# A second load of the keys in groups of 512 columns, and two steps of ScalarE in another order

## What is computed

```python
mix = concat([o_att, o_conv], -1) @ w_out
x1  = layer_norm(ALPHA * x + gate1 * mix)
h2  = x1 * (1 + scale2) + shift2
q   = (h2 @ w_pq).reshape(T, 8, 2, 128)
s   = einsum('thpd,hpnd->thpn', q, sub_keys)      # merged: h2 @ m, m is 1024 x 2048
sv, si = top_k(s, 16)                             # per head and half
cv, ci = top_k(all 256 sums of the two halves, 16)
e   = expert numbers from si and ci               # 8 heads x 16 = 128 per token
a   = gelu(einsum('thkd,td->thk', peer_u[e], h2))
f   = einsum('thk,thkd->td', softmax(cv) * a, peer_v[e])
y   = layer_norm(ALPHA * x1 + gate2 * f)
```

## Time and profile before

| | |
|---|---|
| median of 3 runs | 3889.26 us (3885.03 to 3895.07) |
| profiled execution, own time | 3891.0 us |
| its span, first to last instruction | 3889.2 us |
| busy: PE, DVE, POOL, ACT | 3238.2, 2493.1, 1497.7, 1229.9 us |
| moved by DMA | 1358.47 MB, mean 349 GB/s |
[...]
| the stage `experts` | from 1028.9 us to the end |

### The profile page before, as it was taken

How to read it: one execution, slowest core, us unless ns; L and a number is a source line. 1 busy time by engine, 2 the same in 40 slices (tenths; PEclk the granted TensorE clock), 3 DMA queues, 4 the chain that set the end, 5 groups by cost and what they waited for, 6 DMA issues and landing times.

```text
span 3889.2 us, 42737 instructions
## 1 busy us (share of the span) xinstructions
PE 3238.2 (83%) x12854; PEld 1538.4 (40%) x12854; DVE 2493.1 (64%) x6184; ACT 1229.9 (32%) x3482; POOL 1497.7 (39%) x1312
## 2 busy tenths in 40 slices
PE   7799988888689978788888787887888878788876
PEld 6444656666334433333333333333333333333322
DVE  2111246666378858777877777776776777668975
ACT  2110025555224323333323333233332233323332
POOL 0000003555223324444445444444544445444342
PEclk9899999999899989999999999999999999999999
DMA  9512137889779999999999999999999999999997
GB/s 379 201 38 48 49 115 256 293 309 311 274 306 355 360 414 417 420 420 420 419 413 412 404 420 420 420 399 420 420 403 420 420 400 419 420 420 415 418 412 297
DMA packets 278038, 1358.47 MB, mean 349 GB/s; under 512 B 38153, under 2 KB 59482, under 8 KB 140600
## 3 DMA queue, kind: packets, MB, share of 16 engines
q0 software_dynamic: 171648, 1170.53, 74.3%
q1 hardware_dynamic: 75412, 149.11, 10.8%
q10 hardware_dynamic: 30756, 36.20, 2.7%
HBM read 1330.96 MB, written 24.77 MB: 349 GB/s over the span
## 4 chain that ended last, share of the span: by engine, by line
DMA 37%; PE 21%; DVE 8%; issue 3%; ACT 2%; POOL 2%; ACTq 0%; DVEq 0%; POOLq 0%; SPq 0%
DMA sb_early<-in_uv,sb_experts 28%; PE psum L1599 15%; DMA sb_late<-in_uv,sb_experts 8%; DVE sb_early L1899 4%; PE psum L1552 3%; PE psum L1585 3%; POOL sb_early L1523 2%; DMA sb_rows<-x_scratch 1%; DVE sb_late L1899 1%; ACT sb_diag L1686 1%; DMA x_scratch<-sb_h2T 1%; ACT sb_expert_w L1678 1%; ACT sb_gelu L1675 0%; POOL sb_late L1523 0%; DVE sb_ci L1807 0%
## 5 line engine op out<-in xcount | busy, mean ns | idle before, releaser
L1599 PE MATMUL psum<-sb_early,sb_diag 128*128 128x512 f32 x3376 | 1574.4, 611 | 391.8 <-ACT sb_diag L1686 391.5
L1523 POOL DMA_INDIRECT sb_early<-in_uv,sb_experts x844 | 1008.9, 1195 | 1195.6 <-PE psum L1599 1047.5
L1899 DVE CUSTOM_DVE_ANT_0 sb_early<-sb_early,sb_h 128x1024 f32<-128x1024 f32 x844 | 1027.2, 1226 | 469.9 <-DMA sb_early<-in_uv,sb_experts 435.5
L1599 PEld LDWEIGHTS psum<-sb_early,sb_diag 128*128 128x128 f32 x3376 | 628.3, 193 | 1313.4 <-issue 674.3
L1675 ACT ACTIVATE sb_gelu<-sb_dots 128x2 f32<-128x2 f32 x528 | 107.4, 203 | 1780.1 <-DVE sb_dots L1899 1779.1
L1599 PE MATMUL psum<-sb_late,sb_diag 128*128 128x512 f32 x848 | 399.7, 615 | 103.8 <-ACT sb_diag L1686 103.6
L1523 POOL DMA_INDIRECT sb_late<-in_uv,sb_experts x212 | 253.4, 1195 | 377.7 <-PE psum L1599 270.2
L921 POOL DMA_INDIRECT sb_v_pages<-in_cache_v,sb_v_row_of x240 | 229.3, 955 | 435.8 <-PE psum L948 214.8
L1686 ACT ACTIVATE sb_diag<-sb_ident,sb_expert_w 128x128 f32<-128x128 f32 x1024 | 355.2, 394 | 16.7
L1899 DVE CUSTOM_DVE_ANT_0 sb_late<-sb_late,sb_h 128x1024 f32<-128x1024 f32 x212 | 258.1, 1226 | 130.2 <-DMA sb_late<-in_uv,sb_experts 123.4
L1599 PEld LDWEIGHTS psum<-sb_late,sb_diag 128*128 128x128 f32 x848 | 159.2, 195 | 338.5 <-issue 169.8
(11 more groups left out here) (251 smaller groups left out, 3094.7 us busy)
## 6 DMA issues: line engine op xcount, KB each, us to landing
sb_low<-in_cache_k SPq DMA_DIRECT2D x256, 256.0 KB, 3.0
sb_w_ada<-in_w_ada SPq DMA_DIRECT2D x12, 2048.0 KB
sb_early<-in_uv,sb_experts POOLq DMA_INDIRECT x844, 16.9
sb_w_pq<-in_w_pq ACTq DMA_DIRECT2D x4, 2048.0 KB, 27.4
merged_scratch<-sb_merged ACTq DMA_DIRECT2D x8, 1024.0 KB
sb_early<-merged_scratch SPq DMA_DIRECT2D x8, 1024.0 KB, 26.1
sb_w_bcu<-in_w_in SPq DMA_DIRECT2D x12, 512.0 KB, 6.9
sb_low<-in_w_in ACTq DMA_DIRECT2D x2, 2048.0 KB
```

Source lines behind the costliest of these rows:

```text
L1523: pool.indirect_dma_start(ring(n), None, uv, bass.IndirectOffsetOnAxis(ap=e_all[:, t % 2, k + s:k + s + 1], axis=0))\
L1599: ins = nc.tensor.matmul(psum[:, 2 * (t % 2) + n, :], diag[:, q % CHAINS, s, :], ring(q * PAIR + s)[:, D + n * BANK:D + (n + 1) * BANK], s ...
L1899: nc.vector.tensor_tensor_reduce(u, u, h[:, t % 2, :], 1.0, 0.0, ALU.mult, ALU.add, dots[:, q % CHAINS, s:s + 1]).then_inc(T["dots_ready"], 1)
```

## The change

The second load is made of four groups of 512 columns; each has three DMAs (four k in w_out's space, two in o_att's, two in o_convT's), in which each partition gets 4, 2 and 2 pieces of 512 floats, and a semaphore of its own. PE waits for group n at b = 4 + n. On ACT `mix_copy(1)` comes ahead of `mix_deviation(0)`.

```diff
-        m_land, m_back = sem("pr_m_land"), sem("pr_m_back")
+        m_land, m_back = sem("pr_m_land"), [sem(f"pr_m_back{n}") for n in range(4)]
@@ SP, at t == TILES
                         sp.wait_ge(T["mix_psum"], TILES + 1)
-                        for k in range(KD):
-                            sp.dma_start(m_late[k], m_v[:, k]).then_inc(m_back, 16)
+                        for n in range(4):
+                            cols = slice(n * BANK, (n + 1) * BANK)
+                            for dst, k, many in ((w_flat, 0, 4), (att_flat, 4, 2), (conv_flat, 6, 2)):
+                                sp.dma_start(dst[:, :, cols], m_v[:, k:k + many, cols]).then_inc(m_back[n], 16)
@@ PE, scores(b, part), part == 0
-                        if b == 4:
-                            pe.wait_ge(m_back, 16 * KD)
+                        if 4 <= b < 8:
+                            pe.wait_ge(m_back[n], 48)
@@ ACT, start of the stage
                 mix_root(1)
+                mix_copy(1)
                 mix_deviation(0)
-                mix_copy(1)
                 mix_root(BEFORE)
```

## The result

The changed kernel takes 3908.77 us, the median of 5 runs (3901.81 to 3917.55), against 3888.19 us of the kernel before beside it (5 runs, 3885.03 to 3895.07). The ratio is 1.005 with an interval of [1.0036, 1.0064]: 0.5% slower, and 1.0 us above the forecast of 3907.8.

The account below looks back on a forecast made before the run. Bound taken: the keys' last byte landing, then x1's store, tile 1's load and hidden_made(1). +18.6 for the stall and -0.1 for ACT's order give +18.5 on 3889.3, 3907.8 us; own range 3906 to 3911, 8 in 10 3898 to 3913.

Parts of the forecast that it names:

- Turns by packet: DMA queues alternate by packet, so 2 KB key pieces beside 8 KB gathers get 2 in 10, 84 of 420 GB/s.
- The stall's length: Keys land at 1423.6, then store and load of tile 1; hidden_made(1) starts at 1428.4, not 1409.75: +18.6 us.
- Nothing made up: After hidden_made(1) the whole pattern moves by 18.6 us, with 0 us made up later.
- Part 2: ACT's new order starts mix_product(1, 0) 4.0 us sooner, but scores(0, 0) waits for the first key load: gain 0.1 us.
- The 1.7 us that the prediction calls the clock's: PE's eight matmuls after a short idle may take 1.7 us more or nothing; taken as 0, upper bound +1.7.
- SP's issues: SP is held up issuing 12 DMAs with four times the descriptors; only the store stands behind, which must queue anyway.
- The sum: Whole kernel: +18.6 for the stall less 0.1 for ACT's order gives +18.5 us, 3907.8 us.
- equal bytes: Rival: both queues get the same bandwidth, keys land at 1400.6 as now, kernel takes 3889 or 3891 us; 9%.
- turns of 4 KB: Rival: turns hold two 2 KB pieces, keys get 1/3, 140 GB/s; +14.8 to +17.8 us, 3904 to 3907; 7%.
- the delay made up: Rival: DVE's three gather waits after the stall vanish, 6.9 us together, leaving +11.6, 3901 us; 7%.
- part 1's grouping or its semaphores: Key load in groups of 512 columns: four semaphores in place of one and PE's waits at b = 4 to 7 cost nothing.

Follow-up runs that it names:

- e5: Kernel before, with SP issuing the store of x1's last tile and load of tile 1 ahead of the second key load: 3891.03 us, ratio 1.0005.
- e2: Kernel before with only ACT's new order, mix_copy(1) ahead of mix_deviation(0), second load unchanged: 3889.71 us, ratio 0.9999.
- e7: Changed kernel with only groups 0 and 1 of the second load, half the keys, output not the reference's: 3892.62 us, a single run.
- e4: Kernel before with its second load in two groups of 1,024 columns (4 KB pieces), one semaphore: 3906.56 us, ratio 1.0045.
- e3: Kernel before with its second load in 32 DMAs of 512 columns (2 KB pieces), old order, one semaphore: 3909.81 us, ratio 1.0054.
- e6: Changed kernel with the store of x1's last tile and load of tile 1 ahead of the grouped second key load: 3893.61 us, ratio 1.0008.

## Why the prediction was right, and where it was loose

**Turns by packet** (right). Beside gathers of 8 KB the count is equal in both queues, to 1%, at 2, 4 and 8 KB: 1626 to 1623, 447 to 451, 118 to 118. The share forecast was a fifth, measured 0.21 to 0.22 (84 GB/s forecast, 89 to 90 measured).

**The stall's length** (right): +18.6 us forecast, +18.45 measured. On the axis of before the last keys landed at 1424.0 (forecast 1423.6), the store at 1424.3 (1408.18 + 10.17 + 5.93; forecast 1424.9), and the load of tile 1 took 3.82 us (forecast 3.4). The gap between keys and store was 0.3 us, not 1.3; with the load's 0.4 more these nearly cancel. Two terms inside the keys' landing were off and cancel as well, which is luck. The forecast has the last byte at 1421.5 and its landing seen 2.1 us later. In the trace of after, SP's queue still moves five packets between 1417.5 and 1418.0 (1423.4 to 1423.9 on the axis of before), and the landing at 1418.1 follows within 0.6 us. The last byte thus comes some 2 us later than worked out: on the axis of before the gathers end at 1416, not 1413, and the keys, which then move alone at 401 GB/s (1412 to 1416 in the trace of after), fall to 152 GB/s from 1416.5 on and to 49 from 1417.0. The 2.1 us had been read from a load of 512 KB as if all of them lay behind its last byte; its first packet moves only some 0.9 us after its issue at 1101.5.

**Nothing made up** (right). DVE's first wait for a gather after the stall came at 1510.97, that is 1516.90 against 1497.69: +19.2. Timeline of SP's queue, after, the first and the last store of a tile's `y`:

```profile
1611.44 0.34 SPq L1507 DMA_DIRECT2D out_y_prompt<-sb_rows  x1
...
3874.39 0.33 SPq L1507 DMA_DIRECT2D out_y_prompt<-sb_rows  x1
```

Before they stood at 1598.36 and 3861.86, so the shift is +19.0 and +18.5 (each 5.93 added). The 0.7 us over the stall's 18.45 in front is PE's at low clock: after an idle of 43.34 us the granted clock is 0.50 for 3.4 us (1428.63 to 1432.03), and 0.62 over its eight matmuls. Before it was 0.70 over the same eight, after an idle of 12.64 us. PE, before and after:

```profile
1416.11 5.22 PE L1599 MATMUL psum<-sb_early,sb_diag 128*128 128x512 f32 x8 [12.64 <-ACT sb_diag L1686]
...
1428.63 5.89 PE L1601 MATMUL psum<-sb_early,sb_diag 128*128 128x512 f32 x8 [43.34 <-ACT sb_diag L1688]
```

The prediction's reason for this was too narrow, though. It took the chain through `hidden_made(1)` for the bound and saw slack in the DMA engines at a few places; it did not see that the stretch as a whole moves at 416 GB/s before, a rate that none of these runs exceeds over it. Its arithmetic held because it went to the slower side, where the chain is the longer of the two. The same method would have forecast 13 us of gain for e5, where there is none.

**Part 2** (right). 0.1 us was forecast, and no run can tell the gain from none. PE did start its product 4 to 5 us sooner and then waited for the first load. The 1.7 us that the prediction calls the clock's are the difference of the two rows, and the trace of before shows the clock there: 0.50 from 1922 to 1924, behind the idle of 2.30 us, and 1.00 from 2324.62 to 2328.30, behind that of 2.32. Taken as 0 with 1.7 as the bound, they were hidden in the changed kernel, where they fell on the matmuls ahead of the wait for the first load, and paid in e2 and e7; which of the two happens was not foreseen and is left open.

**SP's issues** (right on what stands behind them; no size was given). SP is held up to 11.8 us by one issue, and its twelve take 57.6 us (1350.51 to 1408.13), where the eight before took 3.9 (1356.44 to 1360.29). That costs nothing here, since the store has to land behind the keys anyway (e4).

**The sum.** +18.5 forecast. The traces show +18.5 at the last store of a tile's `y`; the medians differ by 20.6 us, and the ratio's interval is 14 to 25. That the median came within 1.0 us of 3907.8 is closer than these runs can tell, and in part luck. The forecast's own range has a small slip at its ends: by its terms +17 should be +17.6 (0.9 us less at 426 GB/s, the rate before from 1380 to 1400) and +21.5 should be +21.2 (1.0 and 1.7 more). The rivals: equal bytes and turns of 4 KB fell with e4, the delay made up with the stores of `y`; part 1's grouping or its semaphores as cause fell with e3.

## What to carry to other kernels

Before cutting a load into pieces so that its first part lands sooner, ask who shares the DMA engines with it and with what row size, and what small transfer stands behind it on its own queue: here pieces of 2 KB beside gathers of 8 KB got 21% of the bytes instead of a half, and nobody waited for the first part, while a store of 128 KB did wait for the last. In the stretch here, which moved bytes at 416 GB/s, DVE's stall of 13.53 us cost nothing (e5 is within 0.2% without it), while in the changed kernel the wait grew by 18.45 us with the DMA engines partly idle, and the stretch by 19.0. So hold a stretch's bytes, at the rate measured in it, against the chain before pricing a wait; where e5 shortened the chain alone, by 25 us of wait, and left the bytes as they were, nothing was won.

## What the runs showed of the hardware

- POOL's gathers (software queue, rows of 8 KB) and SP's loads (hardware queue) moved packets in equal number, to within 1%, with SP's rows of 2, 4 and 8 KB: 1626 to 1623 (after, 1364 to 1400), 447 to 451 (e4, 1370 to 1382), 118 to 118 (before, 1372 to 1376). SP's queue got 89 GB/s with 2 KB (3.20 MB in 36 us) and 210 with 8 KB (0.84 MB in 4 us), the gathers 329 and 210, and the sum stayed: 418 and 420 GB/s.
- An issue of the keys on SP took 0.38 us as the first of the second load and up to 11.79 as its sixth (changed kernel, behind 1,792 pieces of 2 KB in five DMAs; 10.86 at the fifth in e4, behind 1,536 pieces of 4 KB in four).
- After a short idle the granted clock sometimes fell and sometimes didn't: it fell after 2.37 us (0.68, 5.30 us for eight matmuls, changed kernel) and 2.89 us (0.68, 8.80 us for sixteen, e2) and not after 2.38 (1.00, 3.60 us for eight, e2). At one and the same place, near 1481 us and after 1.86 us of idle, sixteen matmuls took 7.22 us before and 8.83 in e2 (granted clock 1.00 and 0.57 in their first 3.5 us). What decides it is left open.
- That e5 and e6 take the same time as the kernel before to within 0.2%, the one without a stall of 13.5 us, the other with a new one of 16.6 us, I had not expected when I forecast the change.
